# Weight sums in a seven-product matmul scheme: a narrower wait, and two of the four sums one entry later

## The chip, the cores and the metric

The kernel runs on one core of one Trainium2 chip. The metric is the device time in microseconds (us). Three runs of the kernel before gave 2075.37, 2076.05 and 2077.6 us; their median is 2076.05 us.

TensorE multiplies matrices, VectorE (DVE in the rows) and ScalarE (ACT) work element by element, GpSimd (POOL) does small things, and SyncE (SP) issues the loads of weights. Each engine takes its own instructions in order, and they wait for one another through semaphores.

## The reference

One input of 256 tokens x 2048 columns goes through two transformer layers in float32. What matters here is that nearly all of the time goes into products of 256 tokens with large weight matrices:

```python
h = rmsnorm(x, norm_mix_g[l]);  proj = h @ w_in[l]                  # 2048 x 6144
x = x + mixed @ w_o[l]
xq, xk, xv = hx @ w_xq[l], hm @ w_xk[l], hm @ w_xv[l]               # cross attention
x = x + xo @ w_xo[l]
x = x + (jax.nn.silu(hf @ w_gate[l]) * (hf @ w_up[l])) @ w_down[l]  # 2048 x 5632 and back
...
mod = jax.nn.silu(c) @ w_ada + b_ada                                # second layer
proj = h @ w_in
g = jax.nn.sigmoid(h @ w_merge + b_merge)
merged = g_a * (y_a @ w_br_attn) + g_p * (y_p @ w_br_pool)
return x + gate[:, None] * rmsnorm_2(merged @ w_out, post_g)
```

## The kernel before, in words

**Panels, entries, parts.** A weight matrix is cut into panels of 512 columns. A panel is worked through in pieces of 256 rows x 512 columns, which lie in SBUF as 128 x 1024 (`raw`, eight places). TensorE does not multiply float32 numbers directly here: ScalarE rounds a piece to its high part (`whi`, line 1691), VectorE subtracts that from the raw piece and gets the low part (`wlo`, line 2446), and TensorE makes three products for each pair of operands: high x high, low weights x high, high weights x low (lines 1110 to 1112). A piece made ready in this way is an entry. Entries are numbered through the whole program. There are four places for `whi` and `wlo`, so ScalarE makes a high part when TensorE has finished the entry four before it.

**Pairs of panels.** Two panels that follow one another are mostly taken as a pair, of which there are 40. For the first 512 rows of a pair the kernel uses a scheme with seven products in place of eight (Strassen's), named M1 to M7. For it, four of the entries are not loaded weights but sums or differences of two raw pieces, written over one of the two (line 2458, in `sum_weights`). The table `PRODUCTS` and `_pair` give the order of the entries. With four chunks of rows, as 39 of the pairs have it, the entries of a pair begin thus (a dash is an ordinary entry):

```
0 M5   1 M3   2 -   3 M1   4 -   5 M6   6 M2   7 -   8 -   9 M7   10 -   11 M4
```

The pair `e`, the last third of the feed-forward block (its two panels have three chunks), has M2 at 4, M6 at 5, an ordinary entry at 6, M7 at 7 and M4 at 9. The sums are those of M5, M6, M7 and M4, in this order. The sum of M6 overwrites the piece that M3 was split from, the sum of M7 the one of M1, the sum of M4 the one of M2. The sum of M5 overwrites a piece that has not been split before.

**What sets the order.** `Stream` writes out one list of steps, and each engine's program walks through it. On VectorE, `make` produces the low parts: before the low part of entry n it runs the additions for `w_ada` (line 2076), if any are due there, and then the sum that `sums_before[n]` names. Other work of VectorE (jobs such as the parts of the attention or of the turned activations) comes between two steps of the list, and so between two low parts. So the table `sums_before` sets where in VectorE's queue a sum stands, and by `_loads` also when a place in `raw` comes free for SyncE's next load.

**Names in the rows.** Line 1778 makes the low part `bl` of an activation chunk that TensorE has turned and ScalarE has copied (line 1171) and rounded (line 1181, `bh`). Lines 1790 to 1795 make the four sums of activations that the scheme needs, line 1200 their high parts on ScalarE (`fbh`), line 1799 their low parts (`fbl`). Line 1826 (`difference`) takes a difference of two partial results, for which M7 waits. Lines 2113, 1804 and 2117 finish a gated product of the feed-forward block; line 1757 makes a low part straight from PSUM. Line 2018 splits the second input (`mem`), line 1907 adds a result to the residual, line 1869 copies a result.

Of the kernel before, what the change touches and what calls it, by code (L numbers as in the profile page):

```python
# [222 lines left out]
class Stream:  # L223
# [90 lines left out]
    def _pair(self, f, s):  # L314
        q = len(self.pairs)
        self.role[f], self.role[s] = (0, q), (1, q)
        chunks = len(self.panels[f].rows)
        b22, b12, b11, b21 = (self._item(*which) for which in ((f, 0, 1), (f, 0, 0), (s, 0, 0), (s, 0, 1)))
        todo = iter([(c, hf) for c in range(1, chunks) for hf in range(2)])
        at = {}  # L320

        def normal(p, c, hf, **more):
            n = self._entry(self._item(p, c, hf))
            self._step(n, p, c, hf, tiles=(0, 1), end=(c == chunks - 1 and hf == 1), **more)

        def product(form, place, add=None, minus=False, **more):
            at[form] = n = self._entry(place, add, minus)
            panel, tile, _, half, _ = PRODUCTS[form]
            self._step(n, (f, s)[panel], 0, half, (tile,), form, **more)

        product("M5", b12, b11, start=True, job=False)
        product("M3", b22, start=True, job=False)
        normal(f, *next(todo), snap=("s5", q))
        product("M1", b11, start=True, job=False)
        if chunks == 4:
            normal(f, *next(todo), snap=("s1", q))
            product("M6", b22, b12)
            product("M2", b21, start=True, snap=("v", q))
            normal(f, *next(todo))
            normal(f, *next(todo))  # L340
        else:
            product("M2", b21, start=True, snap=("s1", q))
            product("M6", b22, b12)
            normal(f, *next(todo), snap=("v", q))
        product("M7", b11, b22, minus=True)
        normal(f, *next(todo), snap=("s3", q))
        product("M4", b21, b22, aside=q)
        for c, hf in todo:
            normal(f, c, hf)
        todo = {"u": self._early, "d": self._early, "m": self._late}.get(self.panels[s].kind, [])  # L350
        for i, (c, hf) in enumerate((c, hf) for c in range(1, chunks) for hf in range(2)):
            if i < {"d": 5, "m": 6}.get(self.panels[s].kind, 4):
                self._add_ada(todo)
            normal(s, c, hf)
        self.pairs.append(((f, s), at))

        early = 1 if self.panels[f - 1].stagger == "first" else 2
        for form, n in (("M5", at["M5"] - early), ("M6", at["M3"] + 1), ("M7", at["M1"] + 2),
                        ("M4", max(at["M2"], at["M6"]) + 1)):
            self.sums_before[n] = at[form]  # L360

    def _places(self):
# [80 lines left out]
def build_program(nc, a, out):  # L443
    with ExitStack() as ctx:
        def sb(name, shape, dt=F32):
            return ctx.enter_context(nc.sbuf_tensor(name, shape, dt))

        s = {name: ctx.enter_context(nc.semaphore(f"s_{name}")) for name in SIGNALS}
# [4 lines left out]
        at = {"a": (sb("ah", [P, 16, S], F32R), sb("al", [P, 16, S], F32R)),  # L453
              "b": (sb("bh", [P, 16, S], F32R), sb("bl", [P, 16, S], F32R))}
# [23 lines left out]
        stream = Stream(panel_groups(a))  # L478
        panels, index, role = stream.panels, stream.index, stream.role

        def place(item):

            return raw[:, stream.place[item], :]

        def loaded(item):

            return s[f"raw{stream.place[item]}"], 16 * stream.nth_load[item]
# [1234 lines left out]
        def vector_program(e):  # L1722
            jobs, aside, soon = Jobs(), Jobs(), Jobs()
            count = {name: 0 for name in SIGNALS}
            def done(ins, name="dve"):

                count[name] += 1
                ins.then_inc(s[name], 1)
                return count[name]
# [705 lines left out]
            def make(upto):  # L2435

                nonlocal made
                while made < min(upto, stream.total):
                    n, made = made, made + 1
                    for item in stream.ada_before.get(n, ()):  # L2440
                        add_ada(item)
                    if n in stream.sums_before:
                        sum_weights(stream.sums_before[n])
                    hi, lo = split_at(n)
                    e.wait_ge(s["hi"], n + 1)
                    done(e.tensor_tensor(lo, place(stream.entries[n].item), hi.bitcast(F32), ALU.subtract), "lo")  # L2446

            def sum_weights(n):

                item, add, minus, nth = stream.entries[n]  # L2450
                assert nth == count["t_sum"] + 1
                for one in (item, add):
                    e.wait_ge(*loaded(one))
                if count["lo"]:
                    e.wait_ge(s["lo"], count["lo"])
                if count["t_sum"]:
                    e.wait_ge(s["t_sum"], count["t_sum"])
                done(e.tensor_tensor(place(item), place(add), place(item), ALU.subtract if minus else ALU.add), "t_sum")  # L2458
# [228 lines left out]
```

## Time and profile before

The profiled execution took 2076.66 us; its span, from the first instruction to the last, was 2074.9 us at a mean granted TensorE clock of 0.999.

| engine | busy us | share of the span | instructions |
|---|---|---|---|
| TensorE, matmuls | 2055.9 | 99% | 9334 |
| TensorE, weight loads | 1698.9 | 82% | 9334 |
| VectorE | 1672.5 | 81% | 1835 |
| ScalarE | 1182.0 | 57% | 1534 |
| GpSimd | 54.1 | 3% | 86 |

| work | instructions | busy us | mean ns of one |
|---|---|---|---|
| low parts of weights, line 2446, VectorE | 836 | 1010.1 | 1220 |
| high parts of weights, line 1691, ScalarE | 836 | 877.6 | 1058 |
| sums of raw weights, line 2458, VectorE | 160 | 195.7 | 1223 |

To read it: TensorE is the engine that is nearly always busy, so a change in VectorE's work counts only where TensorE stands still for it. A busy TensorE in these rows does not mean one at its peak, since a matmul's record (390 ns for 512 columns) is longer than the distance to the next one (227 ns).

### The profile page before, as it was taken

How to read it: one execution, taken by the hardware profiler on the slowest of the kernel's cores; microseconds unless marked ns; L12 is line 12 of the kernel's file. 1: busy time of each engine (PE TensorE's matmuls, PEld its weight loads, DVE VectorE, ACT ScalarE, POOL GpSimd, SP SyncE). 2: the span in 40 equal slices, each digit the busy share in tenths (PEclk: the TensorE clock that was granted, in tenths of full speed). 3: DMA queues.
4: the chain of work that ended last, by engine and by line, in shares of the span. 5: the costliest groups of instructions: out<-in, count | busy, mean ns of one | idle time of the engine just before them, and what ended most of it. 6: DMA issues, size and time to landing. Idle time of an engine off the chain costs nothing.

```text
span 2074.9 us, 25392 instructions
## 1 busy us (share of the span) xinstructions
PE 2055.9 (99%) x9334; PEld 1698.9 (82%) x9334; DVE 1672.5 (81%) x1835; ACT 1182.0 (57%) x1534; POOL 54.1 (3%) x86
## 2 busy tenths in 40 slices
PE   9999999999999999999999999999999999999998
PEld 7888888788888888888888888888788888888786
DVE  6777778876766788998889988898777768988875
ACT  6666656755555565555555555555656655654453
POOL 1000000000000000000000000000000000000000
PEclk9999999999999999999999999999999999999999
DMA  9555557655544458777777777776465566889662
GB/s 344 172 177 188 183 174 260 203 192 178 191 163 153 157 178 303 258 265 246 237 238 255 262 244 239 237 263 220 158 214 179 177 204 233 266 289 326 220 202 103
DMA packets 218955, 453.75 MB, mean 219 GB/s; under 512 B 14400, under 2 KB 16592, under 8 KB 218704
## 3 DMA queue, kind: packets, MB, share of 16 engines
q1 hardware_dynamic: 212928, 432.07, 62.2%
q0 software_dynamic: 5616, 19.94, 3.1%
q8 instruction: 74, 1.21, 0.2%
q14 instruction: 49, 0.40, 0.1%
q10 hardware_dynamic: 288, 0.13, 0.0%
HBM read 447.88 MB, written 4.19 MB: 218 GB/s over the span
## 4 chain that ended last, share of the span: by engine, by line
PE 88%; issue 6%; DVE 4%; ACT 1%; DMA 0%; POOL 0%; DVEq 0%; ACTq 0%; POOLq 0%
PE ps L1110 27%; PE ps L1112 27%; PE ps L1111 27%; PE ps L687 2%; DVE wlo L2446 2%; PE ps L837 1%; PE ps L817 1%; DVE raw L2458 0%; PE ps L921 0%; PE ps L963 0%; PE ps L952 0%; PE ps L901 0%; ACT junk L1141 0%; DMA FR<-in_x_t_dram 0%; ACT whi L1691 0%
## 5 line engine op out<-in xcount | busy, mean ns | idle before, releaser
L2446 DVE TENSOR_TENSOR wlo<-raw,whi 128x1024 fp32r<-128x1024 f32 x836 | 1010.1, 1220 | 254.9 <-ACT whi L1691 248.7
L1691 ACT ACTIVATE whi<-raw 128x1024 fp32r<-128x1024 f32 x836 | 877.6, 1058 | 574.6 <-PE ps L1112 524.5
L1110 PE MATMUL ps<-whi,ah 128*128 128x512 f32 x1610 | 638.2, 396 | 5.7 <-DVE wlo L2446 5.6
L1112 PE MATMUL ps<-whi,al 128*128 128x512 f32 x1610 | 627.8, 390 | 0.0
L1111 PE MATMUL ps<-wlo,ah 128*128 128x512 f32 x1610 | 626.8, 389 | 0.0
L1110 PEld LDWEIGHTS ps<-whi,ah 128*128 128x128 f32 x1610 | 302.4, 188 | 68.9 <-DVE wlo L2446 4.8
L1112 PEld LDWEIGHTS ps<-whi,al 128*128 128x128 f32 x1610 | 302.2, 188 | 64.3
L1111 PEld LDWEIGHTS ps<-wlo,ah 128*128 128x128 f32 x1610 | 302.6, 188 | 61.0 <-issue 0.2
L1110 PE MATMUL ps<-whi,bh 128*128 128x512 f32 x854 | 338.1, 396 | 3.0 <-issue 1.6
L1112 PE MATMUL ps<-whi,bl 128*128 128x512 f32 x854 | 333.0, 390 | 0.0
L1111 PE MATMUL ps<-wlo,bh 128*128 128x512 f32 x854 | 332.5, 389 | 0.0
L2458 DVE TENSOR_TENSOR raw<-raw 128x1024 f32<-128x1024 f32 x160 | 195.7, 1223 | 26.6 <-DVE wlo L2446 26.6
L1110 PEld LDWEIGHTS ps<-whi,bh 128*128 128x128 f32 x854 | 160.4, 188 | 38.2 <-issue 4.5
L1112 PEld LDWEIGHTS ps<-whi,bl 128*128 128x128 f32 x854 | 160.3, 188 | 34.0
L1111 PEld LDWEIGHTS ps<-wlo,bh 128*128 128x128 f32 x854 | 160.5, 188 | 33.2 <-issue 1.0
L2076 DVE SCALAR_TENSOR_TENSOR FR<-raw,Z,FR 128x1024 f32<-128x1024 f32 x90 | 114.9, 1277 | 0.0
L1110 PE MATMUL ps<-whi,fah 128*128 128x512 f32 x208 | 83.6, 402 | 0.0
L1112 PE MATMUL ps<-whi,fal 128*128 128x512 f32 x208 | 81.2, 390 | 0.0
L1111 PE MATMUL ps<-wlo,fah 128*128 128x512 f32 x208 | 81.1, 390 | 0.0
L1219 ACT ACTIVATE side<-ps 128x512 f32<-128x512 f32 x120 | 70.8, 590 | 17.8 <-PE ps L1112 17.8
L1804 DVE TENSOR_TENSOR FR<-ps,side 128x512 f32<-128x512 f32 x81 | 53.1, 683 | 7.3 <-PE ps L1112 7.2
L2498 POOL TENSOR_TENSOR Z<-Z 128x2 f32<-128x2 f32 (+1 forms) x18 | 14.8, 825 | 1436.8 <-DVE Z L1740 757.9
(261 smaller groups left out, 1348.1 us busy)
## 6 DMA issues: line engine op xcount, KB each, us to landing
raw<-in_w_in_dram SPq DMA_DIRECT2D x168, 512.0 KB, 4.5
raw<-in_w_ada_dram SPq DMA_DIRECT2D x96, 512.0 KB, 4.6
raw<-in_w_gate_dram SPq DMA_DIRECT2D x88, 512.0 KB, 4.9
raw<-in_w_up_dram SPq DMA_DIRECT2D x88, 512.0 KB, 5.2
raw<-in_w_down_dram SPq DMA_DIRECT2D x88, 512.0 KB, 5.3
raw<-in_w_merge_dram SPq DMA_DIRECT2D x64, 512.0 KB, 5.0
raw<-in_w_o_dram SPq DMA_DIRECT2D x32, 512.0 KB, 4.6
raw<-in_w_xk_dram SPq DMA_DIRECT2D x32, 512.0 KB, 4.6
```

The costliest lines, as they stand in the source:

```text
L687: ins = e.transpose(T[b].ap[:, kk * 256 + t * 128:kk * 256 + t * 128 + 128], src[:, t, (2 * b + kk) * 128:(2 * b + kk + 1) * 128], ident[: ...
L817: ins = e.matmul(A[0].ap[:, t * S:(t + 1) * S], QTC[:, d, t * 128:(t + 1) * 128], XKT[:, 4 * h + d, :], start=(d == 0), stop=(d == 3))
L837: ins = e.matmul(A[b].ap[:, dd * S:(dd + 1) * S], XV[:, k, c0:c0 + 128], PTC[:, k, :], start=(k == 0), stop=(k == 1))
L1110: e.matmul(o, xh[:, k, tokens], wh, start=first, stop=False, skip_group_check=more)
L1111: e.matmul(o, xh[:, k, tokens], wl, start=False, stop=False, skip_group_check=more)
L1112: ins = e.matmul(o, xl[:, k, tokens], wh, start=False, skip_group_check=more, stop=kk == 1 and (st.end or st.form in READ))
L1219: done(e.activation(side_of(pair[place[0]], place[1]), bank_of(pair[panel], t)[:, :], ACT.Copy), "snap")
L1691: done(e.activation(split_at(n)[0], place(item), ACT.Copy), "hi")
L1804: return e.tensor_tensor(dst, src, side_of(p, t), side_op(p))
L2076: done(e.scalar_tensor_tensor(acc, src, csilu[:, k:k + 1], acc, ALU.mult, ALU.add), "ada")
L2446: done(e.tensor_tensor(lo, place(stream.entries[n].item), hi.bitcast(F32), ALU.subtract), "lo")
L2458: done(e.tensor_tensor(place(item), place(add), place(item), ALU.subtract if minus else ALU.add), "t_sum")
```

## The change

Two things are edited. In `_pair`, the sum of M6 is made ahead of the low part of the second entry after M3, not of the first, and the sum of M4 likewise one entry later. In `sum_weights`, a sum no longer waits for all low parts that VectorE has begun before it, but only for the last one made of the piece that the sum overwrites; the sum of M5 then has no such wait. The waits for the loads and for the sum before stay.

```diff
@@ _pair
         early = 1 if self.panels[f - 1].stagger == "first" else 2
-        for form, n in (("M5", at["M5"] - early), ("M6", at["M3"] + 1), ("M7", at["M1"] + 2),
-                        ("M4", max(at["M2"], at["M6"]) + 1)):
+        for form, n in (("M5", at["M5"] - early), ("M6", at["M3"] + 2), ("M7", at["M1"] + 2),
+                        ("M4", max(at["M2"], at["M6"]) + 2)):
             self.sums_before[n] = at[form]
@@ sum_weights
-                if count["lo"]:
-                    e.wait_ge(s["lo"], count["lo"])
+                split_last = max((m for m in range(n) if stream.entries[m].item == item), default=None)
+                if split_last is not None:
+                    e.wait_ge(s["lo"], split_last + 1)
                 if count["t_sum"]:
                     e.wait_ge(s["t_sum"], count["t_sum"])
```

The line numbers of the kernel after are larger by one from here on: its sums are line 2459.

First place, on VectorE: the pair of the second gate panel and the second up panel (`g` 1 and `u` 1), in which the first turned chunk of the hidden layer becomes ready. Before:

```order
L2446 TENSOR_TENSOR wlo<-raw,whi 128x1024 [waits s_hi] x2
L2458 TENSOR_TENSOR raw<-raw 128x1024 [waits s_lo,s_t_sum,s_raw6,s_raw5]
L2446 TENSOR_TENSOR wlo<-raw,whi 128x1024 [waits s_hi] x2
L2458 TENSOR_TENSOR raw<-raw 128x1024 [waits s_lo,s_t_sum,s_raw6,s_raw0]
L2446 TENSOR_TENSOR wlo<-raw,whi 128x1024 [waits s_hi]
L1778 TENSOR_TENSOR bl<-FR,bh 128x1024 [waits s_a_hi]
L2446 TENSOR_TENSOR wlo<-raw,whi 128x1024 [waits s_hi]
L1790 TENSOR_TENSOR FR<-FR 128x2x128 [waits s_a_lo]
```

After:

```order
L2446 TENSOR_TENSOR wlo<-raw,whi 128x1024 [waits s_hi] x2
L2459 TENSOR_TENSOR raw<-raw 128x1024 [waits s_lo,s_t_sum,s_raw5,s_raw6]
L2446 TENSOR_TENSOR wlo<-raw,whi 128x1024 [waits s_hi] x3
L1778 TENSOR_TENSOR bl<-FR,bh 128x1024 [waits s_a_hi]
L2459 TENSOR_TENSOR raw<-raw 128x1024 [waits s_lo,s_t_sum,s_raw5,s_raw0]
L2446 TENSOR_TENSOR wlo<-raw,whi 128x1024 [waits s_hi]
L1790 TENSOR_TENSOR FR<-FR 128x2x128 [waits s_a_lo]
```

The sum of M4 has moved from two places ahead of line 1778 to just behind it. The same happens in the pairs of `g` 5 and `g` 9.

Second place, on VectorE: the pair `e`. Before:

```order
L2458 TENSOR_TENSOR raw<-raw 128x1024 [waits s_lo,s_t_sum,s_raw2,s_raw3]
L2446 TENSOR_TENSOR wlo<-raw,whi 128x1024 [waits s_hi]
L2113 SCALAR_TENSOR_TENSOR FR<-ps3,Z,FR 128x512 [waits s_gated,s_half]
L1804 TENSOR_TENSOR FR<-ps2,side 128x512 [waits s_snap,s_half]
L2117 SCALAR_TENSOR_TENSOR FR<-FR,Z 128x512 [waits s_ev10]
L2446 TENSOR_TENSOR wlo<-raw,whi 128x1024 [waits s_hi] x2
L2458 TENSOR_TENSOR raw<-raw 128x1024 [waits s_lo,s_t_sum,s_raw3,s_raw5]
L2446 TENSOR_TENSOR wlo<-raw,whi 128x1024 [waits s_hi]
L1757 TENSOR_TENSOR bl<-ps4,bh 128x512 [waits s_st_hi]
L2458 TENSOR_TENSOR raw<-raw 128x1024 [waits s_lo,s_t_sum,s_raw3,s_raw7]
L2446 TENSOR_TENSOR wlo<-raw,whi 128x1024 [waits s_hi] x2
```

After:

```order
L2113 SCALAR_TENSOR_TENSOR FR<-ps3,Z,FR 128x512 [waits s_gated,s_half]
L1804 TENSOR_TENSOR FR<-ps2,side 128x512 [waits s_snap,s_half]
L2117 SCALAR_TENSOR_TENSOR FR<-FR,Z 128x512 [waits s_ev10]
L2459 TENSOR_TENSOR raw<-raw 128x1024 [waits s_lo,s_t_sum,s_raw5,s_raw3]
L2446 TENSOR_TENSOR wlo<-raw,whi 128x1024 [waits s_hi] x2
L2459 TENSOR_TENSOR raw<-raw 128x1024 [waits s_lo,s_t_sum,s_raw3,s_raw7]
L2446 TENSOR_TENSOR wlo<-raw,whi 128x1024 [waits s_hi]
L1757 TENSOR_TENSOR bl<-ps4,bh 128x512 [waits s_st_hi]
L2446 TENSOR_TENSOR wlo<-raw,whi 128x1024 [waits s_hi]
L2459 TENSOR_TENSOR raw<-raw 128x1024 [waits s_lo,s_t_sum,s_raw3,s_raw0]
```

The sum of M6 has moved behind lines 2113 to 2117, the sum of M4 behind one more low part.

## Rows read from the trace of the kernel before

**Rows 1.** The page: its first line, and part 1 (busy us, share, instructions).

```profile
span 2074.9 us, 25392 instructions
...
PE 2055.9 (99%) x9334; PEld 1698.9 (82%) x9334; DVE 1672.5 (81%) x1835; ACT 1182.0 (57%) x1534; POOL 54.1 (3%) x86
```

**Rows 2.** The waits of TensorE: who, for whom: us in total, times, longest.

```profile
PE ps L1110 <- DVE wlo L2446: 7.0, 9, 2.7
```

**Rows 3.** The waits of all engines, the row of the sums; columns as above.

```profile
DVE raw L2458 <- DVE wlo L2446: 26.6, 130, 0.6
```

**Rows 4.** VectorE in order of time, pair of g 1: start, us, what, [idle before <-releaser].

```profile
817.94 1.23 DVE L2446 TENSOR_TENSOR wlo<-raw,whi 128x1024 fp32r<-128x1024 f32 x1 [0.49 <-ACT whi L1691]
819.36 1.22 DVE L2458 TENSOR_TENSOR raw<-raw 128x1024 f32<-128x1024 f32 x1 [0.20 <-DVE wlo L2446]
820.51 1.22 DVE L2446 TENSOR_TENSOR wlo<-raw,whi 128x1024 fp32r<-128x1024 f32 x1
822.65 1.23 DVE L1778 TENSOR_TENSOR bl<-FR,bh 128x1024 fp32r<-128x1024 f32 x1 [0.93 <-ACT bh L1181]
823.80 1.22 DVE L2446 TENSOR_TENSOR wlo<-raw,whi 128x1024 fp32r<-128x1024 f32 x1
...
828.38 1.21 DVE L1799 TENSOR_TENSOR fbl<-FR,fbh 128x1024 fp32r<-128x1024 f32 x1
829.52 3.48 DVE L2446 TENSOR_TENSOR wlo<-raw,whi 128x1024 fp32r<-128x1024 f32 x3
```

**Rows 5.** ScalarE in order of time, the same pair.

```profile
821.56 1.06 ACT L1181 ACTIVATE bh<-FR 128x1024 fp32r<-128x1024 f32 x1
...
826.76 1.06 ACT L1200 ACTIVATE fbh<-FR 128x1024 fp32r<-128x1024 f32 x1 [2.24 <-DVE FR L1795]
```

**Rows 6.** TensorE in order of time, around four of its waits.

```profile
396.42 0.47 PE L1110 MATMUL ps<-whi,bh 128*128 128x512 f32 x1 [0.70 <-issue]
...
830.06 0.39 PE L1112 MATMUL ps<-whi,fal 128*128 128x512 f32 x1
830.79 0.50 PE L1110 MATMUL ps<-whi,ah 128*128 128x512 f32 x1 [0.34 <-DVE wlo L2446]
...
1429.74 0.47 PE L1110 MATMUL ps<-whi,fbh 128*128 128x512 f32 x1 [0.28 <-DVE side L1826]
...
1512.24 0.39 PE L1112 MATMUL ps<-whi,fal 128*128 128x512 f32 x1
1512.93 0.47 PE L1110 MATMUL ps<-whi,ah 128*128 128x512 f32 x1 [0.31 <-DVE wlo L2446]
1513.24 0.39 PE L1111 MATMUL ps<-wlo,ah 128*128 128x512 f32 x1
```

**Rows 7.** VectorE in order of time, pair e.

```profile
1416.29 0.75 DVE L2113 SCALAR_TENSOR_TENSOR FR<-ps,Z,FR 128x512 f32<-128x512 f32 x1 [0.34 <-PE ps L1112]
...
1420.90 1.22 DVE L2458 TENSOR_TENSOR raw<-raw 128x1024 f32<-128x1024 f32 x1 [0.20 <-DVE wlo L2446]
...
1428.91 0.68 DVE L1826 TENSOR_TENSOR side<-ps,side 128x512 f32<-128x512 f32 x1
```

**Rows 8.** VectorE in order of time, pair of the first two xk panels.

```profile
383.63 1.22 DVE L2458 TENSOR_TENSOR raw<-raw 128x1024 f32<-128x1024 f32 x1 [0.20 <-DVE wlo L2446]
...
391.24 1.23 DVE L2458 TENSOR_TENSOR raw<-raw 128x1024 f32<-128x1024 f32 x1 [0.20 <-DVE wlo L2446]
...
395.11 1.21 DVE L2446 TENSOR_TENSOR wlo<-raw,whi 128x1024 fp32r<-128x1024 f32 x1
```

**Rows 9.** VectorE in order of time, pair of q 0 and ga 0.

```profile
1510.42 1.22 DVE L2458 TENSOR_TENSOR raw<-raw 128x1024 f32<-128x1024 f32 x1 [0.20 <-DVE wlo L2446]
1511.57 1.22 DVE L2446 TENSOR_TENSOR wlo<-raw,whi 128x1024 fp32r<-128x1024 f32 x1
```

**Rows 10.** Stretches: us, busy of each engine (instructions), clock, DMA share, GB/s.

```profile
820.00:825.00 5.00, 5.00 (x25) 4.14 (x25) 4.07 (x5) 3.56 (x4) 0.00 (x0) 1.00 0.60 192
...
835.00:840.00 5.00, 5.00 (x24) 4.14 (x23) 5.00 (x6) 2.12 (x2) 0.00 (x0) 1.00 1.00 343
```

## The prediction, made before the run

> **What bounds the kernel now.** I read the page first, then who waits for whom, then the order of time around each of TensorE's waits, and last the order of VectorE's instructions before and after. The page says that TensorE is busy for 2055.9 of 2074.9 us [rows 1]. So 19.0 us are all that could be gained without making its own work shorter, and they include the start and the tail. Its waits say where VectorE is behind that idle time: 9 waits for a low part, 7.0 us, of which the longest, 2.7 us, is the start [rows 2]. That leaves about 4.3 us. (By the distance between matmuls each such wait costs a little more than the idle time shown, since a record is longer than the distance to the next: at 830.79 the row shows 0.34 us of idle time, while the matmul comes 0.73 us after the one before it, where 0.23 is usual [rows 6].) Everything else in this change plays on VectorE, which has slack nearly everywhere. The question is therefore only what moves at those few places where TensorE waits for VectorE, and whether new ones appear.
>
> **Part 1: the narrower wait.** In the trace, 130 of the 160 sums stand idle for the end of the low part just ahead of them, together 26.6 us, about 0.20 us each [rows 3]. The price in VectorE's time is a bit higher, because two instructions without such a wait overlap: three low parts in a row take 3.48 us where one takes 1.22, so they begin (3.48 - 1.22) / 2 = 1.13 us apart, and the low part at 820.51 begins 1.15 us after the sum (I take 1.14); the sum at 819.36 begins 1.42 us after the low part at 817.94 [rows 4]. So a wait costs 1.42 - 1.14 = 0.28 us, and all 130 of them about 36 us of VectorE. After the change no sum stands directly behind the low part that it waits for (that is what the move of M6 and M4 does; M7 already had one entry between; M5 has no such wait left), so I take all of them as gone. The Trainium skill speaks against this: in "VectorE: DVE Perf Modes", section "The DRAIN you can't avoid", it says that the semaphore costs nothing extra between VectorE instructions, since the pipe has to empty anyway. By that the wait would return nothing. This trace disagrees, with 1.42 against 1.14 us between starts [rows 4]; the skill's copies are of another size, so I keep it as a rival below. On the path, only those waits count that stand in an unbroken run of VectorE's work which ends in a wait of TensorE.
>
> **Part 2: a sum one entry later.** It takes 1.14 us of VectorE wherever it stands. If VectorE works without a break before and after, the move gives the low part ahead 1.14 us and takes nothing from what follows. If the entries behind are early, nothing changes. It costs where the sum leaves a spot from which VectorE then waits for another engine, and lands behind that wait, in a run that TensorE waits for. The order shows two kinds of such places.
>
> First, the pair of `g` 1. Before, the sum of M4 starts at 819.36; then come a low part and an idle time of 0.93 us, in which VectorE waits for ScalarE's rounding, which ends at 821.56 + 1.06 = 822.62 [rows 4, 5]. From line 1778 at 822.65 to the low part at 829.52 VectorE works without a break (the lines left out in rows 4, as in rows 7 and 8, carry no idle time but that of the sums) [rows 4], and TensorE waits for that low part: it ends at 830.74, and the matmul comes at 830.79 [rows 4, 6]. In the new order the sum stands behind line 1778. ScalarE's rounding depends on TensorE's transposes and does not come earlier. So the whole run from 823.80 on is late by one sum, 1.14 us. Does something else in it give way? Line 1799 needs ScalarE's `fbh`, ready at 826.76 + 1.06 = 827.82, and starts at 828.38 [rows 4, 5]; but `fbh` itself hangs on line 1795, in the same run, and shifts with it. Nothing gives way, and no wait of 0.20 us is in the run to be saved. Cost +1.14 us. The same pattern stands in the pairs of `g` 5 and `g` 9: three in all, +3.42 us.
>
> Second, the pair `e`. VectorE waits for TensorE until 1416.29 and then works on without a break but for one wait of a sum, at 1420.90, to line 1826 at 1428.91 [rows 7]; M7 on TensorE is released by that difference and starts at 1429.74, after idle time [rows 6]. Before, the sum of M6 stood ahead of 1416.29, in the shadow; now it stands behind lines 2113 to 2117: +1.14. The wait at 1420.90 goes: -0.28. The sum of M4 was in this run and stays in it: 0. Together +0.86 us, and since TensorE already waits there, all of it counts.
>
> **Part 3: what is gained.** In the first pair of `xk`, VectorE works without a break until 395.11, and TensorE's matmul at 396.42 waits for that low part [rows 6, 8]. The two waits ahead of it, at 383.63 and 391.24 [rows 8], go: -0.56 us. The low part behind the sum of 383.63 comes 1.42 us earlier, but its gain is given back at the next low parts, behind which the sum then stands. In the pair of `q` 0 the low part at 1511.57 stands behind the sum at 1510.42 [rows 9] and comes 1.42 us earlier. TensorE lost 1513.24 - 1512.24 - 2 x 0.227 = 0.55 us there [rows 6], and that is all that can be gained: -0.55 us. The other waits (the start, the first forms of each block, the single panels) stand behind sums of M5, which do not move, or behind none: 0.
>
> **Part 4: the loads.** Which load takes which place in `raw` changes, the order of loads does not. In most pairs a place is free about 1.1 us later. In the pairs of `g` 1, 5 and 9 the raw pieces of M4's sum come free at 825.0 (the shifted sum's end, 823.80 + 1.22) in place of 820.6 [rows 4]. The DMA engines are busy for 0.60 of that time and for 1.00 of the time from 835 on [rows 10], so there is room just there. I cost it at 0; what hides it is the stock of loaded pieces. Bounds: no less than 0, as nothing is loaded earlier by it; at most another 1.1 us at each of the three places.
>
> **The sum.** +3.42 + 0.86 - 0.56 - 0.55 = +3.2 us. The profiled execution took 2076.66 us, its span 2074.9 us [rows 1]; that would make 2079.8. The median of the three runs is 0.6 us lower, 2076.05, so I state 2076.05 + 3.2 = 2079.2 us. The other 130 or so waits, some 30 us of VectorE, are in stretches where TensorE does not wait and show nowhere but in VectorE's idle time.
>
> **The rivals.**
> A. Not slower: the sum that lands behind line 1778 and lines 2113 to 2117 is absorbed, because TensorE has something else to wait for there, or ScalarE's release comes early enough that the sum fits. Then only the gains are left: 2076.05 - 1.1 = 2074.9 us. It decides when the low part at 829.52 may be over 1 us late without TensorE noticing. Against it: TensorE comes 0.05 us behind that low part. For it: only that waits are matched to releases after the fact. 12%.
> B. The wait returns nothing, since VectorE's distance between the low part and the sum stays at 1.42 us, for the sum still waits for loads and for the sum before it. Then pair `e` costs 1.14, `xk` gains 0, `q` 0 gains 0.55 by the move alone: +3.42 + 1.14 - 0.55 = +4.0, 2080.1 us. The skill's rule on the DRAIN named above would have the same result. 10%.
> C. The late places in `raw` do cost: TensorE meets a piece that has not landed in the busy stretch from 835 on [rows 10], at each of the three places, up to 1.1 us more. 2079.2 + 3.3 = 2082.5 us. Against it: no load is behind any of TensorE's waits now. 10%.
> D. The edit does not do what it says, and VectorE's queue waits as before: then 2076.1 us. The new order contradicts it, and I put it in A's share.
> E. More waits of TensorE than these few melt away, from all the freed VectorE time: at most the 4.3 us of rows 2, 2071.8 us. Three of those waits get longer by my reading, so 3%.
>
> **How the numbers follow.** The forecast has 65%, with a range of its own from 2078 to 2080.6. To hold 8 of 10 the range reaches from 2075.3 to 2082.6, leaving out part of A and E below and the worst of C above. A measurement of this kernel tells 0.2% (4.15 us) from no change: below 2071.9 is faster, above 2080.2 slower. Slower: one in seven of the forecast's share (9%), half of B (5%), C (10%), together 0.24. Faster: E's 3%. The rest, 0.73, is within.
>
> **What would show it.** Right: in the pair of `g` 1, the sum behind line 1778 with no idle time before it, and a gap between TensorE's matmuls ahead of the entry behind M7 of up to 1.9 us in place of 0.73 (part of it already before M7), at three places; the idle time of the sums behind low parts near 0 in place of 26.6 us; M7 of the pair `e` released 0.9 us later. Wrong: TensorE's waits for low parts no longer than before (A), the sums still begin 1.4 us after a low part with 0.20 us of idle time (B), or ScalarE's high parts, and TensorE after them, released by a DMA (C).

## The result, and the profile after

The changed kernel took 2080.2 us, median of 14 runs (2079.18 to 2082.48), against 2076.61 us (14 runs, 2075.37 to 2078.05) for the kernel before on the same chip: 3.6 us more, a ratio of 1.0017 with a 95% interval of 1.001 to 1.0024. The forecast was 2079.2 us, +3.2 us. So the kernel after is slower, by a little less than the 0.2% (4.15 us) that the prediction had set as the border to no change.

First the page of the kernel after, its first line and the busy times; they answer to [rows 1].

```profile
span 2077.4 us, 25353 instructions
...
PE 2056.0 (99%) x9334; PEld 1697.6 (82%) x9334; DVE 1661.2 (80%) x1835; ACT 1183.4 (57%) x1534; POOL 54.2 (3%) x86
```

The profiled execution took 2079.19 us. TensorE's busy time is the same within 0.1 us, the clock too (0.999), so everything that was lost is idle time of TensorE. VectorE is busy for 11.3 us less with the same 1835 instructions, since two that have no wait between them overlap (0.08 us in each of 130 places, as worked out in part 1 of the prediction, make 10.4).

Next, on the same page, the sums and the low parts among the costliest groups: busy time, mean ns of one, and after the second bar the idle time ahead of them. The row of the sums answers to [rows 3].

```profile
L2446 DVE TENSOR_TENSOR wlo<-raw,whi 128x1024 fp32r<-128x1024 f32 x836 | 1007.9, 1221 | 281.6 <-ACT whi L1691 277.6
...
L2459 DVE TENSOR_TENSOR raw<-raw 128x1024 f32<-128x1024 f32 x160 | 194.9, 1218 | 0.0
```

The 130 waits of the sums, 26.6 us, are gone to the last. In their place the low parts wait longer: 281.6 us in all in place of 254.9, and of that 277.6 us in place of 248.7 for ScalarE's high parts. VectorE's freed time was turned into other waiting nearly everywhere.

Then the waits of TensorE's matmuls after: us in total, times, longest. The first row answers to [rows 2].

```profile
PE ps L1110 <- DVE wlo L2446: 6.2, 6, 2.4
...
PE ps L1110 <- DVE side L1826: 2.7, 4, 1.1
...
PE ps L1110 <- ACT side L1219: 0.9, 1, 0.9
```

TensorE waits for a low part 6 times, less often than before, but there are four waits for the difference of line 1826 in place of one (new are three, in the pairs of `g` 1, 5 and 9; the one of the pair `e` was there before). And there is one for line 1219, with which ScalarE copies a partial result out of PSUM (called the snapshot below), and which no step of the prediction named.

Now VectorE in order of time in the pair of `g` 1, which answers to [rows 4].

```profile
821.44 1.23 DVE L1778 TENSOR_TENSOR bl<-FR,bh 128x1024 fp32r<-128x1024 f32 x1 [2.04 <-ACT bh L1181]
822.58 1.22 DVE L2459 TENSOR_TENSOR raw<-raw 128x1024 f32<-128x1024 f32 x1
823.71 1.22 DVE L2446 TENSOR_TENSOR wlo<-raw,whi 128x1024 fp32r<-128x1024 f32 x1
...
828.30 1.22 DVE L1799 TENSOR_TENSOR fbl<-FR,fbh 128x1024 fp32r<-128x1024 f32 x1
829.43 3.49 DVE L2446 TENSOR_TENSOR wlo<-raw,whi 128x1024 fp32r<-128x1024 f32 x3
```

The idle time ahead of line 1778 has grown from 0.93 to 2.04 us: the work ahead of that idle stretch is now shorter by the sum of M4. Line 1778 itself starts 1.21 us earlier on the time axis than before, the low part at the end of the run, for which TensorE waits, only 0.09 us earlier. Between the two, 1.12 us were lost, one sum.

TensorE in the same place, which answers to the second and third row of [rows 6].

```profile
828.53 0.47 PE L1110 MATMUL ps<-whi,fah 128*128 128x512 f32 x1 [0.53 <-DVE side L1826]
...
829.76 0.40 PE L1112 MATMUL ps<-whi,fal 128*128 128x512 f32 x1
830.71 0.50 PE L1110 MATMUL ps<-whi,ah 128*128 128x512 f32 x1 [0.55 <-DVE wlo L2446]
```

The one gap of 0.73 us has become two: one ahead of M7, which waits for line 1826, and one of 0.95 us behind it (829.76 to 830.71, where 0.23 is usual).

VectorE in the pair `e`, which answers to [rows 7]:

```profile
1418.44 0.75 DVE L2113 SCALAR_TENSOR_TENSOR FR<-ps,Z,FR 128x512 f32<-128x512 f32 x1 [0.34 <-PE ps L1112]
...
1420.49 1.22 DVE L2459 TENSOR_TENSOR raw<-raw 128x1024 f32<-128x1024 f32 x1
1421.63 2.35 DVE L2446 TENSOR_TENSOR wlo<-raw,whi 128x1024 fp32r<-128x1024 f32 x2
1423.89 1.22 DVE L2459 TENSOR_TENSOR raw<-raw 128x1024 f32<-128x1024 f32 x1
...
1431.90 0.69 DVE L1826 TENSOR_TENSOR side<-ps,side 128x512 f32<-128x512 f32 x1
```

From line 2113 to line 1826 it takes 13.46 us, 12.62 before: +0.84. The sum at 1423.89 begins 2.26 us after the first of two low parts, 1.13 us each, without the 0.20 us of idle time.

TensorE there and in the pair of `q` 0, which answers to the last four rows of [rows 6]:

```profile
1431.22 0.39 PE L1112 MATMUL ps<-whi,bl 128*128 128x512 f32 x1
1432.73 0.47 PE L1110 MATMUL ps<-whi,fbh 128*128 128x512 f32 x1 [1.13 <-DVE side L1826]
...
1515.17 0.39 PE L1112 MATMUL ps<-whi,fal 128*128 128x512 f32 x1
1515.40 0.39 PE L1110 MATMUL ps<-whi,ah 128*128 128x512 f32 x1
1515.62 0.39 PE L1111 MATMUL ps<-wlo,ah 128*128 128x512 f32 x1
```

M7 of the pair `e` now waits 1.13 us, and the gap at `q` 0 is closed: the matmuls follow 0.23 us apart. On VectorE the sum there stands behind line 1869 now, where [rows 9] had it ahead of the low part:

```profile
1510.82 3.49 DVE L2446 TENSOR_TENSOR wlo<-raw,whi 128x1024 fp32r<-128x1024 f32 x3
1514.23 0.69 DVE L1869 COPY FR<-ps 128x512 f32<-128x512 f32 x1
1514.83 1.22 DVE L2459 TENSOR_TENSOR raw<-raw 128x1024 f32<-128x1024 f32 x1
```

**Where the time went.** The two profiled executions don't begin alike: the first of TensorE's matmuls on weights comes at 10.30 us before and at 9.38 us after. That is 0.92 us in favour of the kernel after. The change is hardly its reason: in the nine traces of the experiments below it lies anywhere from 8.89 to 9.17 us, at 9.00 with the old order of the sums (experiment 2) and at 8.90 with the old wait (experiment 3). The lead of the kernel after over the kernel before, for the same instruction, then runs as follows (a minus: the kernel after is earlier).

| place | before | after | difference | step |
|---|---|---|---|---|
| TensorE, first matmul on weights | 10.30 | 9.38 | -0.92 | |
| pair of `xk`, matmul behind TensorE's wait | 396.42 | 394.94 | -1.48 | -0.56 |
| `g` 1, VectorE, line 1778 | 822.65 | 821.44 | -1.21 | +0.27 |
| `g` 1, VectorE, low part of the last wait | 829.52 | 829.43 | -0.09 | +1.12 |
| pair `e`, VectorE, line 2113 | 1416.29 | 1418.44 | +2.15 | +2.24 (`g` 5, `g` 9) |
| pair `e`, VectorE, line 1826 | 1428.91 | 1431.90 | +2.99 | +0.84 |
| `q` 0, TensorE, second matmul behind the wait | 1513.24 | 1515.62 | +2.38 | -0.61 |
| end of the span | 2074.9 | 2077.4 | +2.5 | +0.1 |

From -0.92 to +2.5 these are 3.4 us, beside 3.6 us between the medians. TensorE's 9334 matmuls of the two traces can also be matched one by one. From 831 to 1083 us (time axis of the kernel before), from 1089 to 1342 and from 1350 to 1428, the distance between the two traces stays the same within 0.05 us, so nothing is lost between the places of the table.

**The first pair of `xk`** has more in it than the table shows. VectorE and TensorE before (TensorE's next wait, behind the one at 396.42), and then TensorE after in the same stretch:

```profile
396.52 1.23 DVE L2458 TENSOR_TENSOR raw<-raw 128x1024 f32<-128x1024 f32 x1 [0.20 <-DVE wlo L2446]
...
399.03 0.47 PE L1110 MATMUL ps<-whi,bh 128*128 128x512 f32 x1 [0.54 <-DVE wlo L2446]
```

```profile
396.76 0.48 PE L1110 MATMUL ps<-whi,bh 128*128 128x512 f32 x1
...
406.66 0.39 PE L1112 MATMUL ps<-whi,bl 128*128 128x512 f32 x1
407.97 0.47 PE L1110 MATMUL ps<-whi,bh 128*128 128x512 f32 x1 [0.93 <-ACT side L1219]
```

The wait at 399.03 is gone too, so that the lead there is 2.27 us, or 1.35 without the start. It had stood behind the sum of M4 (at 396.52), which now comes one entry later. But 11 us on, TensorE waits 0.93 us at the entry of M4 for the snapshot of line 1219, and the lead is given back. ScalarE after shows the chain that ends there:

```profile
387.61 1.06 ACT L1691 ACTIVATE whi<-raw 128x1024 fp32r<-128x1024 f32 x1 [2.42 <-DVE raw L2459]
...
402.45 0.63 ACT L1141 ACTIVATE junk<-FR 128x512 bf16<-128x512 f32 x1 [0.43 <-DMA FR<-in_mem_dram]
...
405.87 0.63 ACT L1141 ACTIVATE junk<-FR 128x512 bf16<-128x512 f32 x1 [0.98 <-DMA FR<-in_mem_dram]
...
407.25 0.58 ACT L1219 ACTIVATE side<-ps 128x512 f32<-128x512 f32 x1
```

ScalarE waits 2.42 us for the moved sum of M6, since it can round M6 only when the sum is made. The squares of `mem` (line 1141, for the mean square of `mem`) stand behind it in its queue, and after them comes GpSimd's request for the next blocks of `mem`, which overwrites what the squares read. They are not late by the whole 2.42 us: before, ScalarE had stood idle for 1.76 us one step further on, for line 1907, and that wait is gone.

```profile
388.81 0.63 ACT L1141 ACTIVATE junk<-X 128x512 bf16<-128x512 f32 x1 [1.76 <-DVE X L1907]
```

What is left is 2.42 - 1.76 = 0.66 us. GpSimd before, and then after:

```profile
395.93 0.70 POOL L2555 DMA_DIRECT2D FR<-in_mem_dram  x1 [69.04 <-ACT junk L1141]
```

```profile
395.68 0.70 POOL L2556 DMA_DIRECT2D FR<-in_mem_dram  x1 [69.70 <-ACT junk L1141]
```

With the start taken off, the request is 0.67 us later than before (-0.25 + 0.92), while TensorE is over a microsecond earlier. So ScalarE meets blocks that have not landed (0.43 and 0.98 us), in front of the snapshot of line 1219.

### The profile page after: what moved, and what is told of

Same layout as the page of the kernel before. It is cut to its first block, busy times and chain, and to the rows that moved or that the text cites. A ratio compares the mean times of both kernels' runs of the same rounds, so it can differ in the third digit from the quotient of the medians.

```text
span 2077.4 us, 25353 instructions
## 1 busy us (share of the span) xinstructions
PE 2056.0 (99%) x9334; PEld 1697.6 (82%) x9334; DVE 1661.2 (80%) x1835; ACT 1183.4 (57%) x1534; POOL 54.2 (3%) x86
## 3 DMA queue, kind: packets, MB, share of 16 engines
q8 instruction: 74, 1.21, 0.2%
## 4 chain that ended last, share of the span: by engine, by line
PE 89%; issue 6%; DVE 3%; ACT 1%; POOL 0%; DMA 0%; DVEq 0%; ACTq 0%; POOLq 0%
PE ps L1110 28%; PE ps L1112 27%; PE ps L1111 27%; PE ps L687 2%; DVE wlo L2446 1%; PE ps L817 1%; PE ps L837 1%; DVE raw L2459 0%; PE ps L921 0%; PE ps L963 0%; PE ps L952 0%; PE ps L901 0%; ACT junk L1141 0%; ACT whi L1691 0%; DMA FR<-in_x_t_dram 0%
## 5 line engine op out<-in xcount | busy, mean ns | idle before, releaser
L2446 DVE TENSOR_TENSOR wlo<-raw,whi 128x1024 fp32r<-128x1024 f32 x836 | 1007.9, 1221 | 281.6 <-ACT whi L1691 277.6
```

## The experiments

Each kernel is compared with the kernel before as it ran beside it, since that gave 2075.2 us beside the kernels below and 2076.6 us above.

**1. The kernel after, with M4 early again in the three pairs.**

```
 _pair, of the kernel after
-                        ("M4", max(at["M2"], at["M6"]) + 2)):
+                        ("M4", max(at["M2"], at["M6"]) + (1 if q in (16, 22, 28) else 2))):
```

> The changed kernel, but in the pairs of g 1, g 5 and g 9 alone (3 of 40) the sum of M4 stands one entry earlier again, as in the kernel before, and so ahead of line 1778 (in that place it stands directly behind the low part it must wait for). Place theory: the cost of the change is one sum of 1.14 us in the unbroken run that starts at line 1778, at three places. Then this kernel is 3.4 us faster than the changed one: 2080.2 - 3.4 = 2076.8 us, +0.2 us against the kernel before (median 2076.6), and the distance between the two matmuls at about 830 us is 0.73 us again at all three places. Rival (the loss is spread: places in raw that come free later, loads bunched, the new order on ScalarE): three pairs of 40 change little, at least 2079 us.

Measured: 2075.67 us (11 runs) beside 2075.23 us (33 runs); ratio 1.0002 [0.9993, 1.0011]. With one number changed in three of 40 pairs the loss of over 3 us is gone down to 0.4 us (0.2 were expected). TensorE of this kernel in the pair of `g` 1:

```profile
828.11 0.39 PE L1112 MATMUL ps<-whi,fal 128*128 128x512 f32 x1
828.84 0.50 PE L1110 MATMUL ps<-whi,ah 128*128 128x512 f32 x1 [0.34 <-DVE wlo L2446]
```

That is the gap of 0.73 us of the kernel before, and there is none ahead of M7. What the three late sums cost is shown, and rival A is out.

**2. The narrow wait alone.**

```
 _pair, of the kernel after
-        for form, n in (("M5", at["M5"] - early), ("M6", at["M3"] + 2), ("M7", at["M1"] + 2),
-                        ("M4", max(at["M2"], at["M6"]) + 2)):
+        for form, n in (("M5", at["M5"] - early), ("M6", at["M3"] + 1), ("M7", at["M1"] + 2),
+                        ("M4", max(at["M2"], at["M6"]) + 1)):
```

> The kernel before with the narrower wait alone: all sums stand where they stood. The sums of M6 and M4 still stand behind the low part that they must wait for, those of M7 and M5 no longer wait. My theory: a wait costs 0.28 us of VectorE and counts only in a run that TensorE waits for: one M7 in the first xk pair (given back there later, because the block of mem that is loaded again sets the end) and one in pair e. So -0.3 us, 2076.3 us, the same within the noise; the sums of M7 start 1.14 us after the low part ahead of them where VectorE has work, in place of 1.42, and M7's release in pair e comes 0.28 us earlier. Rival (the semaphore costs nothing extra on VectorE): the sums of M7 still start 1.42 us after the low part, no TensorE wait changes.

Measured: 2074.59 us beside 2075.23 us; ratio 0.9997 [0.9988, 1.0006]. A difference that small isn't told from none by the time; the trace tells it. VectorE of this kernel in the pair of `g` 1, the sum of M7 and then that of M4:

```profile
810.90 2.35 DVE L2446 TENSOR_TENSOR wlo<-raw,whi 128x1024 fp32r<-128x1024 f32 x2
813.17 1.22 DVE L2459 TENSOR_TENSOR raw<-raw 128x1024 f32<-128x1024 f32 x1
...
816.30 1.22 DVE L2446 TENSOR_TENSOR wlo<-raw,whi 128x1024 fp32r<-128x1024 f32 x1 [0.78 <-ACT whi L1691]
817.73 1.23 DVE L2459 TENSOR_TENSOR raw<-raw 128x1024 f32<-128x1024 f32 x1 [0.20 <-DVE wlo L2446]
```

The sum of M7 no longer waits for the low part just ahead of it and starts 2.27 us after the first of two, 1.14 each. The sum of M4 still does, and starts 1.43 us after it. Both stand in one trace, the instructions are of one size, and only the wait is different. Rival B is refuted: the wait on the instruction ahead costs 0.29 us. The Trainium skill ("VectorE: DVE Perf Modes", "The DRAIN you can't avoid") says, from a row of copies, that the semaphore costs nothing extra; for the instructions here this trace shows otherwise, 1.43 against 1.14 us. In the pair `e` TensorE's gap ahead of M7 shrinks by one such wait, from 0.67 us (1429.07 to 1429.74 before) to 0.38 us:

```profile
1427.38 0.39 PE L1112 MATMUL ps<-whi,bl 128*128 128x512 f32 x1
1427.76 0.47 PE L1110 MATMUL ps<-whi,fbh 128*128 128x512 f32 x1
```

The time came out 0.6 us lower where 0.3 was expected. In the first pair of `xk` the narrower wait of M7's sum was expected to gain 0.28 us and to lose it again. TensorE's matmul at 396.42 comes at 394.84 here, where the first one on weights is at 9.00: 0.28 us earlier with the start taken off. But there is no wait for the snapshot behind it, and the 0.28 us are kept.

**3. The moves alone, with the wait as before.**

```
 sum_weights, of the kernel after
-                split_last = max((m for m in range(n) if stream.entries[m].item == item), default=None)
-                if split_last is not None:
-                    e.wait_ge(s["lo"], split_last + 1)
+                if count["lo"]:
+                    e.wait_ge(s["lo"], count["lo"])
```

> The kernel before with the two moves alone: the sums of M6 and M4 one entry later, and every sum still waits for all low parts begun before it. Place theory: three times +1.14 us behind line 1778, pair e +1.14 us (the wait of M7's sum stays in its run), q 0 -0.55 us, xk 0: +4.0 us, 2080.6 us, a little slower than the changed kernel. The three distances at about 830, 1088 and 1347 us grow in sum by 1.14 us each as in the changed kernel; the wait of TensorE for M7 in pair e grows by 1.14 us against before, where the changed kernel shows 0.85. Rival (the narrower wait is what costs, since sums start earlier and hold up others): near 2076.6 us.

Measured: 2079.96 us beside 2075.23 us; ratio 1.0022 [1.0014, 1.0031]; +4.7 us. The moves are the whole loss, and the narrow wait takes some of it back. VectorE and then TensorE of this kernel in the pair `e`:

```profile
1424.37 1.22 DVE L2458 TENSOR_TENSOR raw<-raw 128x1024 f32<-128x1024 f32 x1 [0.20 <-DVE wlo L2446]
...
1428.67 1.23 DVE L2458 TENSOR_TENSOR raw<-raw 128x1024 f32<-128x1024 f32 x1 [0.20 <-DVE wlo L2446]
```

```profile
1431.39 0.39 PE L1112 MATMUL ps<-whi,bl 128*128 128x512 f32 x1
1433.51 0.47 PE L1110 MATMUL ps<-whi,fbh 128*128 128x512 f32 x1 [1.73 <-DVE side L1826]
```

TensorE's two matmuls are 2.12 us apart, 1.51 us in the kernel after, so here the narrow wait is worth 0.61 us, two waits. What was expected had counted one: in the old order the sum of M4 stood behind line 1757 and did not wait, in the new one it stands directly behind a low part and would. That is 0.3 us of the 0.7 us by which this kernel is above the expected +4.0. The trace shows the other 0.4 us in the first pair of `xk`, which was expected to give 0: TensorE waits 1.2 us for the snapshot there and, with the start taken off, leaves the pair 0.4 us later than in the kernel before. The last block of `mem` took 8.5 us from request to landing in this execution, and 7.5 to 7.9 us in the two of the changed kernel.

**4. Each sum at the better of its places.** The narrow wait; the sum of M6 late in the pair of `q` 0 alone; the sum of M4 as in the kernel before, but in the pair `e` later still, just ahead of M4's own low part (three entries later than in the kernel before).

```
 _pair, of the kernel after
-... ("M6", at["M3"] + 2), ... ("M4", max(at["M2"], at["M6"]) + 2) ...
+... ("M6", at["M3"] + (2 if early == 1 else 1)), ... ("M4", at["M4"] if chunks == 3 else max(at["M2"], at["M6"]) + 1) ...
```

> A version put together from the reading: the narrower wait; the sum of M6 one entry later only in the pair of q 0, as before in all others; the sum of M4 as before in all pairs with four chunks, and in pair e only just ahead of M4's own low part, behind line 1826 (the difference that M7 waits for). Place theory: q 0 -0.55 us; in pair e the run up to line 1826 is shorter by the sum, 1.14 us, and by the wait of M7's sum, 0.28 us, of which TensorE can use no more than what it lost there, about 0.5 us; the three pairs as before; xk 0. Together -1.0 us: 2075.6 us, and against the changed kernel -4.6 us. Rival: M4's high part now has to wait for its sum, and TensorE then waits for M4 in pair e: no gain there, 2076.1 us or more.

Measured: 2073.9 us beside 2075.23 us; ratio 0.9994 [0.9986, 1.0003]; -1.3 us. A second time, as `e9_best_again`, beside another run of the kernel before:

> The best version so far (e4) once more, to have it beside e8 on the same chip: 1.3 us faster than the kernel before, as measured; only the move of M4's sum in the first xk pair differs between the two.

2073.84 us beside 2075.25 us; ratio 0.9994 [0.9985, 1.0003]; -1.4 us. Each interval reaches just over 1, so that it is faster is likely but not shown. The 0.3 to 0.4 us more than expected stand in the first pair of `xk`, where the traces of both show TensorE some 0.25 us earlier, the gain of M7's sum as in experiment 2. In the first of the two, TensorE no longer waits in the pair `e`: on VectorE the sum of M4 stands behind line 1826, which is done at 1426.91. VectorE, then TensorE:

```profile
1426.23 0.68 DVE L1826 TENSOR_TENSOR side<-ps,side 128x512 f32<-128x512 f32 x1
1426.83 1.22 DVE L2459 TENSOR_TENSOR raw<-raw 128x1024 f32<-128x1024 f32 x1
```

```profile
1427.19 0.39 PE L1112 MATMUL ps<-whi,bl 128*128 128x512 f32 x1
1427.42 0.39 PE L1110 MATMUL ps<-whi,fbh 128*128 128x512 f32 x1
```

**5. The changed kernel without the second load of `mem`.** The reading above of the first pair of `xk` rests on the blocks of `mem` that land late. Here blocks 2 and 3 are not loaded at all.

```
 ScalarE's squares of mem, of the kernel after
-                    e.wait_ge(s[f"mt{j % 2}"], 16 * (j // 2 + 1))
+                    e.wait_ge(s[f"mt{j % 2}"], 16)
...
 GpSimd's program, of the kernel after
-            for j in range(2, 4):
-                e.wait_ge(s["m_sq"], 2 * (j - 1))
-                e.dma_start(MT[j - 2], mem_v[:, :, j * PW:(j + 1) * PW]).then_inc(s[f"mt{j - 2}"], 16)
```

> The changed kernel, but the mean squares of mem are taken twice over its first two blocks of 512 columns, and blocks 2 and 3 are not loaded (this changes that part of the computation: the root mean square of mem covers half of its columns). In the changed kernel TensorE reaches entry 155 0.56 us and entry 156 1.35 us ahead of the kernel before (counted from each run's first entry), and stands still for 1.28 us before entry 160, M4, for a snapshot that ScalarE makes after the squares of mem's last block, which landed at 405.8. Theory (the loads of mem give the xk gain back): without them the stop before entry 160 is gone, and the 1.3 us stay: 1.3 us faster than the changed kernel of the same call. Rival (M4's late sum or its high part is what holds entry 160, or ScalarE is simply full): TensorE still stands before entry 160 for about 1.3 us, and the time is that of the changed kernel.

**6. M6 early in the first pair of `xk` alone.**

```
 _pair, of the kernel after
-... ("M6", at["M3"] + 2) ...
+... ("M6", at["M3"] + (1 if q == 7 else 2)) ...
```

> The changed kernel, but in the first xk pair alone the sum of M6 stands one entry earlier, as before. In the changed kernel ScalarE waits 2.42 us for this sum at its high part of M6, and the squares, the request for mem's blocks 2 and 3 and their landing all come about 0.7 us later than in the kernel before (counted from the first entry). Theory: here ScalarE does not wait, mem's last block lands 0.7 us earlier, TensorE's wait for the snapshot before entry 160 goes, but TensorE stands before entry 151 for the low part behind the sum again; in the end the kernel is 0 to 0.3 us faster than the changed one. Rival (the landing does not hang on ScalarE's wait): the landing and the wait before entry 160 stay as in the changed kernel.

**7. The changed kernel again, beside these two.**

> The changed kernel once more, beside the others of this call: 3.6 us slower than the kernel before, as measured. All my readings count on the same differences in every execution: the three pairs +1.14 us each, pair e +0.85, q 0 -0.55, xk about 0, so 3.2 to 3.9 us. Against: if the first measurement was off, it lies elsewhere.

The three ran beside one another and beside the kernel before, which took 2075.22 us (27 runs):

| kernel | median us | ratio, 95% | over before |
|---|---|---|---|
| changed again | 2078.6 | 1.0016 [1.0008, 1.0025] | +3.4 |
| without the second load of `mem` | 2077.64 | 1.0012 [1.0004, 1.0021] | +2.4 |
| M6 early in the first pair of `xk` | 2078.22 | 1.0015 [1.0006, 1.0024] | +3.0 |

Without the load TensorE has no wait left in this pair behind the one at 388.55 us, and the kernel is 1.0 us faster than the changed one (1.3 were expected; the stop for the snapshot was shorter in the changed kernel run beside it). With M6 early, ScalarE rounds M6 without a wait, GpSimd's first request is at 394.68 us (395.54 in the changed kernel run beside it, which began 0.19 us later), ScalarE waits for one block instead of two, and TensorE's wait for line 1219 is gone. GpSimd and then ScalarE of the kernel with M6 early:

```profile
394.68 0.71 POOL L2556 DMA_DIRECT2D FR<-in_mem_dram  x1 [69.03 <-ACT junk L1141]
```

```profile
404.44 0.63 ACT L1141 ACTIVATE junk<-FR 128x512 bf16<-128x512 f32 x1 [0.16 <-DMA FR<-in_mem_dram]
```

So the chain (sum of M6, ScalarE, request, landing, squares, line 1219, TensorE) is shown at both ends: TensorE's wait at its end goes when the load is taken out, and when the sum goes back. How long that wait is hangs on the transfer too, which takes 6.8 to 8.5 us for the last block in the ten traces that have it. By time the second gives 0.4 us only (0 to 0.3 were expected), since two waits of TensorE that the late sum had removed (at 384.88 and 394.88 us) are back.

**8. The best order with M4 late in the first pair of `xk`.**

```
 _pair, of experiment 4
-... ("M4", at["M4"] if chunks == 3 else max(at["M2"], at["M6"]) + 1) ...
+... ("M4", at["M4"] if chunks == 3 else max(at["M2"], at["M6"]) + (2 if q == 7 else 1)) ...
```

> The best version so far (e4), and in the first xk pair the sum of M4 one entry later, behind the low part of entry 156. In the changed kernel this move brought TensorE 0.79 us forward at entry 156, a wait I had not priced, and the run with M6 early in xk kept 1.0 us of it and of M7's wait beyond entry 161. Theory: 0.7 to 0.8 us faster than e4, so 2.0 us faster than the kernel before: ratio 0.9990. Rival (the loads of mem's last blocks take it back here too): as e4, ratio 0.9994, with a wait of TensorE for the snapshot before entry 160.

Measured: 2073.76 us (11 runs, 2072.69 to 2074.69) beside 2075.25 us; ratio 0.9993 [0.9984, 1.0002]. The same order without this move ran beside it (2073.84). TensorE of the latter, and then of this kernel:

```profile
397.45 0.47 PE L1110 MATMUL ps<-whi,bh 128*128 128x512 f32 x1 [0.55 <-DVE wlo L2446]
```

```profile
396.63 0.47 PE L1110 MATMUL ps<-whi,bh 128*128 128x512 f32 x1
```

The wait is gone and 0.8 us with it, and the profiled execution (span 2070.9 us against 2072.2) keeps them. The medians are only 0.08 us apart. So the expected gain is in the trace and not in the time; the profiled execution was the fastest of the 11. The spans of the 11 executions lie from 2070.9 to 2072.6 us, without the move from 2071.9 to 2072.3, so some are faster by the move and others are not. In the profiled one the last block of `mem` landed 7.1 us after its request. The rival, that a later landing takes the gain back, may hold in others. Whether it does is open, as they have no trace.

## Why the prediction was right, and where it was not

**The sum, term by term.** Forecast +3.2 us; the two traces show +3.4 with the start taken off, the medians +3.6.

| term | forecast | trace |
|---|---|---|
| M4 behind line 1778, three pairs | +3.42 | +3.36 (1.12 in `g` 1, 2.24 in the two others) |
| pair `e` | +0.86 | +0.84 |
| first pair of `xk`, up to `g` 1 | -0.56 | -0.29 |
| pair of `q` 0 | -0.55 | -0.6 |
| sum | +3.2 | +3.3, and 0.1 to the end |

**Part 1, the narrow wait,** was right in its size (0.28 us, 0.29 in experiment 2) and in its consequence: 36 us of VectorE freed, and little of it on the path. Experiment 2 gave 0.6 us. Experiment 3 is about 1.3 us above the changed kernel of experiment 7 (+4.7 and +3.4, each against the kernel before that ran beside it); of these, 0.6 are the two waits in the pair `e`, and the rest is in the first pair of `xk`, where the last block of `mem` took 0.9 us longer to land in the one trace than in the other, so that not all of it is the narrow wait's.

**Part 2, the moved sums,** was right in place, mechanism and size. Nothing gave way in the run from line 1778 on: `fbh` shifted with line 1795, from which it is made. Experiment 1 takes back only that and has only the pair's old gap left.

**Part 3, the gains,** is where a step failed, though its number came out near. That the two waits ahead of the matmul at 396.42 go and give -0.56 us happened to the hundredth at that matmul. But the prediction stopped following there. It put the other waits of TensorE at 0, as standing behind sums of M5 or behind none; the next one, at 399.03, stood behind M4's sum, and its going gave 0.79 us more. And it missed that the late sum of M6 makes ScalarE wait 2.42 us in place of 1.76 us, with the squares, the request for `mem` and the snapshot of line 1219 queued behind. It had followed the moved sum on VectorE's queue only, not on ScalarE's, which waits for it. The two misses nearly cancel (-0.79 and, up to `g` 1, +1.06 us); that the term came out near, and the total with it, is luck to this extent. The gain at `q` 0 was right.

**Part 4, the loads,** was costed at 0, which holds: experiment 1, which takes the moved sums of the three pairs back and the later places in `raw` with them, gives back 3.0 to 3.2 us, no more than the 3.4 that the sums alone make, so nothing is left for the loads. The load that did matter is one of GpSimd's, which the part did not speak of.

**The rivals.** A would have left 2074.9 us; the low part did turn out to be on TensorE's path. B's time, 2080.1 us, is nearer to the measured 2080.2 than mine, and would have looked confirmed by it; only the trace (no idle time ahead of any sum, 1.14 us between starts) shows that it is wrong. D is out by the same row. Of E, that other waits of TensorE melt, there is no more than the 0.79 us in the first pair of `xk` (the wait at 386.14 goes too, but its 0.56 us are given back by 394.20, as the prediction had it). C and the loads of weights: none of TensorE's waits after is put down to one, and in the busy stretch from 835 us on the distance between the two traces doesn't move, as said under the table.

## What to carry to other kernels

A piece of work that stands in an idle stretch ahead of a wait costs nothing, and its full length once it is moved behind that wait: before an instruction is moved, look for the nearest idle time ahead of it, and whether the run that it lands in is one that the bounding engine waits for. Freeing 36 us of an engine that is not the bound is worth what stands in a few such runs, here 0.6 us by experiment 2. And when a result is made later, follow all engines that wait for it, with what is queued behind them, their DMA requests too, not only the queue in which it is made.

## What the runs showed of the hardware that was not expected

A wait of VectorE for its own instruction just ahead costs 0.28 to 0.29 us per instruction of 128 x 1024 float32 elements, of which the trace shows 0.20 us as idle time; the rest is overlap that is lost. With another instruction in between, it costs nothing that the trace shows.

The first matmul on weights comes at different times: 9.38 us and 9.17 us in two profiled executions of the changed kernel, 8.97 us and 8.89 us in two of the kernel of experiment 4, 10.30 us in the one of the kernel before. Where differences of 1 us are read from two traces, this has to be taken off first. What makes the difference no run here shows.

One and the same transfer, the last block of `mem`, took from 6.8 us (experiment 4 run again) to 8.5 us (experiment 3) from GpSimd's request to its landing. Where an engine waits for such a landing, differences of 1 us between two traces can be the transfer's alone.
